# Stationary blocks of the feature projections laid out in interleaved pairs and read at a step of two, with moving operand and output traversed backwards

## What is computed

```python
# first block, two layers: a mixer and a convolved feed-forward, on 512 (later 256) tokens
q, k, v, u, g = jnp.split(h_lat @ w_in, splits, axis=-1)          # hybrid attention + gating
y_lat = jnp.concatenate([a_lat, s_lat], axis=-1) @ w_out
q, k, v, g = jnp.split(h_lat @ w_in, splits, axis=-1)             # retention
return (jax.nn.silu(g) * on.astype(g.dtype)) @ w_out
a = dwconv3(h @ w_in, conv_w, conv_b)                             # conv_ffn, D_FF = 2816
gate, up = jnp.split(a, 2, axis=-1)
return (jax.nn.silu(gate) * up) @ w_out

# second block, two layers on 272 tokens: mLSTM + LRU, differential attention, each with an MLP
h = h + _ab_mixer(hn, ab_w_in[j], ...)
h = h + _diff_attn(hn, c_w_in[j], ..., c_w_out[j], lambda_init)
a = jax.nn.relu(hn @ w1)
return (a * a) @ w2
```

## Time and profile before

| | us |
|---|---|
| median of 3 runs | 2000.32 |
| lowest, highest | 1997.08, 2002.23 |
| the profiled execution, whole | 2003.57 |
| its span, first to last instruction | 2001.8 |
| PE busy in it | 1907.4 |
| DVE busy in it | 1239.6 |
| ACT busy in it | 920.6 |

### The profile page before, as it was taken

The page is one execution under the profiler, slowest core; times in us unless marked ns, Lnnn a source line. Parts: engine busy times, 40 slices in busy tenths (PEclk is TensorE's granted clock), DMA queues, the critical chain, the costliest instruction groups (busy, mean ns, idle before and its releaser), DMA issues.

```text
span 2001.8 us, 33468 instructions
## 1 busy us (share of the span) xinstructions
PE 1907.4 (95%) x13373; PEld 1697.0 (85%) x13373; DVE 1239.6 (62%) x1853; ACT 920.6 (46%) x1441; POOL 229.6 (11%) x179
## 2 busy tenths in 40 slices
PE   5999979999999899999899998999999999989998
PEld 3776657778888589999889997998899999879997
DVE  6355355543664546677577768656875567787564
ACT  5344343322332422177475554357553445665453
POOL 2100104430552000022000000000010010000001
PEclk9999989999999999999999999999999999989999
DMA  9611465433222433222445553532345554224553
GB/s 389 239 61 64 168 232 185 166 115 113 91 85 93 183 125 107 89 101 85 168 153 177 198 177 128 176 134 91 127 169 181 177 172 145 95 95 169 192 187 127
DMA packets 43952, 296.79 MB, mean 148 GB/s; under 512 B 4976, under 2 KB 6129, under 8 KB 11697
## 3 DMA queue, kind: packets, MB, share of 16 engines
q1 hardware_dynamic: 36576, 247.48, 35.6%
q10 hardware_dynamic: 6048, 42.50, 5.9%
q0 software_dynamic: 1200, 5.02, 0.7%
HBM read 293.94 MB, written 1.05 MB: 147 GB/s over the span
## 4 chain that ended last, share of the span: by engine, by line
PE 83%; DVE 10%; ACT 4%; issue 2%; DMA 1%; POOL 1%; ACTq 0%; DVEq 0%; POOLq 0%
PE acc L462 23%; PE acc L463 23%; PE acc L464 22%; DVE w_lo L397 2%; PE acc L457 2%; PE acc L459 2%; PE acc L458 2%; PE wk L555 1%; PE wk L1733 1%; ACT w_hi L387 1%; PE acc L1722 1%; PE wk L1462 1%; DVE X L1073 1%; DVE nt L1079 1%; PE acc L1483 1%
## 5 line engine op out<-in xcount | busy, mean ns | idle before, releaser
L397 DVE TENSOR_TENSOR w_lo<-w_raw,w_hi 128x1024 fp32r<-128x1024 f32 (+2 forms) x472 | 574.3, 1255 | 177.2 <-ACT w_hi L387 175.6
L462 PE MATMUL acc<-Hhi,w_hi 128*128 128x272 f32 (+2 forms) x2048 | 654.1, 319 | 20.6 <-DVE Hlo L826 7.6
L387 ACT ACTIVATE w_hi<-w_raw 128x1024 fp32r<-128x1024 f32 (+2 forms) x472 | 452.4, 1005 | 424.3 <-PE acc L464 332.9
L463 PE MATMUL acc<-Hlo,w_hi 128*128 128x272 f32 (+2 forms) x2048 | 637.2, 311 | 0.0
L464 PE MATMUL acc<-Hhi,w_lo 128*128 128x272 f32 (+2 forms) x2048 | 635.8, 310 | 0.0
L462 PEld LDWEIGHTS acc<-Hhi,w_hi 128*128 128x128 f32 x2048 | 389.6, 190 | 67.8 <-issue 39.3
L464 PEld LDWEIGHTS acc<-Hhi,w_lo 128*128 128x128 f32 x2048 | 388.2, 190 | 19.5
L463 PEld LDWEIGHTS acc<-Hlo,w_hi 128*128 128x128 f32 x2048 | 389.1, 190 | 18.1
L462 PE MATMUL acc<-Fhi,w_hi 128*128 128x256 f32 (+2 forms) x864 | 262.6, 304 | 3.2 <-POOL Flo L1152 1.5
L464 PE MATMUL acc<-Fhi,w_lo 128*128 128x256 f32 (+2 forms) x864 | 261.9, 303 | 0.0
L463 PE MATMUL acc<-Flo,w_hi 128*128 128x256 f32 (+2 forms) x864 | 261.9, 303 | 0.0
(11 more groups left out here) (415 smaller groups left out, 2667.0 us busy)
## 6 DMA issues: line engine op xcount, KB each, us to landing
w_raw<-in_w_ffn_in SPq DMA_DIRECT2D x44, 1024.0 KB, 4.8
ada_ring<-in_w_ada ACTq DMA_DIRECT2D x40, 1024.0 KB, 5.8
w_raw<-in_w_mlp_in SPq DMA_DIRECT2D x32, 1024.0 KB, 4.8
w_raw<-in_w_mlp_out SPq DMA_DIRECT2D x32, 1024.0 KB, 4.8
w_raw<-in_w_ffn_out SPq DMA_DIRECT2D x32, 704.0 KB, 4.0
ada_first<-in_w_ada SPq DMA_DIRECT2D x8, 1024.0 KB, 20.4
w_raw<-in_w_ret_v SPq DMA_DIRECT2D x8, 1024.0 KB, 5.0
w_raw<-in_w_ret_g SPq DMA_DIRECT2D x8, 1024.0 KB, 4.7
```

The lines of the kernel that those rows point to most:

```text
L387: act.activation(w_hi[:, r, a:b], w_raw[:, r, a:b], ACT.Copy).then_inc(hi_done, 1)
L397: dve.tensor_tensor(w_lo[:, r, a:b], w_raw[:, r, a:b], w_hi[:, r, a:b].bitcast(F32), ALU.subtract).then_inc(lo_done, 1)
L462: pe.matmul(o, w_hi[:, r, w], x_hi(k), start=k == 0, stop=False)
L463: pe.matmul(o, w_hi[:, r, w], x_lo(k), start=False, stop=False)
```

## The change

For feature projections the host lays the blocks out in pairs: blocks 2i and 2i + 1 share 256 columns, the first on the even ones and the second on the odd ones (`_paired`). `stationary` reads a block back with a step of two elements, so that its 128 columns span 1024 bytes of a row in place of 512; a last block without a partner (K = 11, C = 1) stays as it was. In the same matmuls the moving operand and the output are given from the last column to the first, so each result lands where it did before. Projections of `kind` "tok" keep both. The number of instructions, their order on each engine, the semaphores, the transfers' sizes, the copies of ACT and DVE (still over contiguous halves) and all addresses are unchanged; only lines are renumbered (L462 to L464 become L470 to L472).

```diff
+        def stationary(w, r, p, j):
+
+            if j == p.K * p.C - 1 and j % 2 == 0:
+                return w[:, r, j * P:(j + 1) * P]
+            return w[:, r, j // 2 * 2 * P + j % 2:(j // 2 + 1) * 2 * P:2]
+
...
+                    if p.kind != "tok":
+                        o = o[:, ::-1]
...
-                        w = slice((k * p.C + c) * P, (k * p.C + c + 1) * P)
-                        pe.matmul(o, w_hi[:, r, w], x_hi(k), start=k == 0, stop=False)
-                        pe.matmul(o, w_hi[:, r, w], x_lo(k), start=False, stop=False)
-                        mm = pe.matmul(o, w_lo[:, r, w], x_hi(k), start=False, stop=k == last)
+                        b_hi, b_lo = stationary(w_hi, r, p, k * p.C + c), stationary(w_lo, r, p, k * p.C + c)
+                        pe.matmul(o, b_hi, x_hi(k)[:, ::-1], start=k == 0, stop=False)
+                        pe.matmul(o, b_hi, x_lo(k)[:, ::-1], start=False, stop=False)
+                        mm = pe.matmul(o, b_lo, x_hi(k)[:, ::-1], start=False, stop=k == last)
...
+def _paired(w, blocks):
+
+    n = w.shape[0]
+    pairs = w[:, :, :blocks // 2 * 2 * P].reshape(n, P, blocks // 2, 2, P).transpose(0, 1, 2, 4, 3)
+    return np.concatenate([pairs.reshape(n, P, -1), w[:, :, blocks // 2 * 2 * P:]], 2)
...
+    for p in PROJ:
+        if p.kind != "tok":
+            arrays["w_" + p.name] = _paired(arrays["w_" + p.name], p.K * p.C)
```

## The result

| | before | changed |
|---|---|---|
| median, us | 2001.28 (4 runs) | 2026.34 (4 runs) |
| lowest, highest | 1997.08, 2002.40 | 2025.84, 2026.68 |
| ratio | 1 | 1.0136, 95% interval 1.0118 to 1.0154 |
| profiled execution: span, us | 2001.8 | 2024.8 |

A forecast was written before the change was run, and what follows sets the result against it. PE's streaming was taken as the bound; gains of 10.3, 2.6, 2.4, 14.6 and 0.4 us summed to 30.3, step and reversal at zero. Keeping 30 gave 1970 us (chance 0.35), range 1910, less 2, to 2045, the forecast's own 1955 to 1990.

The forecast's parts named there:

- What bounds the kernel: Whole kernel: PE streams, busy 1907.4 of 2001.8 us with 83% of the chain, so the time is a sum of pitches.
- the price of 10.3 us for each ns: The three feature-projection matmuls, L462 to L464: each ns on the pitch of all 10320 was priced at 10.3 us.
- The source of the surplus: PE's matmuls: the 6 to 11% above array pace was put down to moving-operand reads colliding with the next weight load.
- The first rival: Feature matmuls: the whole gap to plain fp32's pace vanishes, 102 us of which 90 kept, 1910 us; chance 0.15.
- The step of two "at no cost of its own": Weight loads of feature matmuls: reading every second element was taken to add zero, hidden under the moving stream.
- The 1150 matmuls that ran at 113.4: 256-column matmuls in ffn1_in0 after its pause and both mlp1_out, taken as already at the good pace, with no gain.
- the third rival: Feature matmuls: loads touching twice the lines meet the stream more, +30 us and +5 us, 2035 us; chance 0.20.
- Equal pace keeps the streams apart: Load and moving stream, both over 1024 bytes per pitch at 256 columns, should stay apart; good pace everywhere, 30.3 us gained.
- The reversal "at zero": Feature matmuls: descending reads and accumulator writes touch the same bytes in the same number, so were priced at zero.
- The 512-wide matmuls: Feature matmuls of 512 columns: taken as already at the good pace, 226.6 ns; only 192 at 228.9 gain, 0.4 us.
- The fourth rival: Feature matmuls: the stationary read (+341 us, 2340 us) or the backward stream (+74 us) becomes the bound; chance 0.17.
- The two paces: 256-column matmuls: 113.4 and 117.8 ns for the same instructions, read as good and bad meetings; one pace, 113.4, expected afterwards.

## Why the prediction was wrong

**What bounds the kernel: right.** PE streams; both medians moved as its pitches did, and no other engine took or gave anything. The method of reading pitches from windows carried over to each experiment, and so did the price of 10.3 us for each ns on all 10320 matmuls.

**The source of the surplus: wrong, and this is the step on which the sign hung.** The prediction took all of the surplus over plain fp32's pace for meetings of the moving stream with the weight load. A plain fp32 matmul of 256 columns takes 3.45 / 16 = 0.216 us, nearly twice the time of an fp32r one, so it takes in moving columns at half the rate; it could not show what the fp32r stream costs by itself. Two experiments show more. With a load that walks nowhere the surplus stayed (228.7 ns), and with a moving operand that walks nowhere it went (215.9). Of the 13 ns above the array's 213.3, 11 come with the walk of the moving operand. Whether that walk costs them by itself or against any weight load, even one that does not walk, stays open. The first rival (the surplus goes entirely, 1910 us) had put its own counter-argument rightly: 226.6 looked like a property of the stream. It was less constant than it was taken for, though: the projections at 512 columns ahead of ffn0_in0 averaged 227.3 to 231.3 ns in the trace of before.

**The step of two "at no cost of its own": a term mis-sized.** The bound was written down, 110 ns for an open load, with the remark that from 3% more the 256-wide pitch follows it. These 110 ns are no measure of the load, only a ceiling: the matmuls in that row are plain fp32, and at the rate of the earlier trace rows 128 columns of it take 108 ns by themselves. With a moving operand of one element the step takes the pitch from 111.6 to 117.8, 5.6% more. The argument for zero was that the moving stream reads 1024 bytes in the time in which the load reads 512; but that is a contiguous read, and does not show what a read with a step costs. The 1150 matmuls that ran at 113.4 went to 117.8, which is the 5 us that the third rival had for them. In the changed kernel this can't be put down to the step alone, since the reversal alone brought them to 117.8 too.

**Equal pace keeps the streams apart: wrong.** With the step alone the 256-wide pitch is 119.9 ns, above the load's own 117.8 and above both paces of before, and at 512 columns, where the load is hidden nearly twice over, the stream slowed by 7 ns. If equal pace helped, the 256-wide pitch would have come down. Two streams do disturb each other here: the step of the load slows the 512-wide stream when it walks (233.5 ns) and not when it reads one element (215.9). But they disturb each other more at a wider span, not less.

**The reversal "at zero": wrong by 7 ns at 512 columns,** and by 4 ns at 256 in mlp1_out1 (113.5 to 117.8). It is the read of the moving operand; the write is free, as the prediction had it for both.

**The 512-wide matmuls were taken for immune.** They were given 0.4 us of the forecast, and the third rival, whose sign and size came nearest (2035 us, measured 2026), gave them next to nothing either. They carry 12.8 of the 24.9 us. So that rival's place was half wrong: it had the whole loss at 256 and 272 columns. Its mechanism, more meetings of the stream with a load that spans more, is what the step alone shows at 512.

**The fourth rival** priced a load at half as much again (2340 us). With a step of two and a moving operand of one element the load is the bound at 117.8 ns, 6 ns over the contiguous kernel and not 50; with a step of four it is the bound at about 233 ns, and the kernel took 2826 us. Its other half, 5% for reading backward, came out at 3% at 512 columns.

**The two paces.** The prediction expected a single pace afterwards, and there is a single one in both ffn1_in halves, but the slow one. That in the kernel before they come and go between executions is a guess: its median in the batches lay between 2000.4 and 2004.0 us with single runs from 1995.2 to 2007.6, while the four runs of the changed kernel lie within 0.9 us. Such a spread would fit, but no second trace of one kernel tests it.

**Still open** is why both edits together cost less (1.36%) than the step alone (1.5%). The traces show where: 117.8 ns against 119.9 at 256 columns, 126.3 against 127.5 at 272 (in mlp0_out both have 126.7). How the direction of the stream and the span of the load interact there was not tried apart. Nor was it settled why a step of two in the load slows a 512-wide stream by the same amount as a backward read, and both by no more.

## What to carry to other kernels

Before a surplus is put down to two streams that collide, take each away in turn, by an operand that reads one element over and over; two kernels of that kind show here that the surplus follows the moving operand, and that a step in the load costs time. As a working rule from these runs, a matmul's pitch is the larger of the stream's (226.6 ns for 512 fp32r columns, in proportion below) and the load's (at most 111.6 ns for 128 contiguous columns), with a few ns, up to 7, for their company; at 256 columns these are 2 ns apart, so anything that touches the layout of the stationary block has to be priced against the load as well. Keep fp32r stationary blocks contiguous and read the moving operand forward; the direction of the output was free here.

## What the runs showed of the hardware

- A weight block of 128 fp32r columns loads in at most 111.6 ns contiguous, 117.8 at a step of two (both with a moving operand of one element), about 233 at a step of four.
- A moving fp32r operand of 512 columns streams in 226.6 ns forward, 233.5 backward, and 215.9 where all columns are one element, each with a weight load of 128 columns beside it.
- A step of two in that load takes the forward stream to 233.5 ns, and leaves the stream of one element at 215.9.
- The output of a matmul may be written from the last column to the first at no cost (ratio 1.0000).
- A PE that is busy by its records can still lose its clock. In the two kernels with narrow matmuls the granted clock fell to 0.50, the level of 1.2 GHz, for long stretches, in which matmuls of 256, 64 and 64 columns took turns and PE's records covered all of the time. Part 2 of the page of the contiguous one, and a window of it (width, PE, PEld, DVE, ACT, POOL, PEclk):

```profile
PEclk7889778555565599955555555557955999975999
```

```profile
1150.00:1190.00 40.00, 40.00 (x190) 40.00 (x190) 18.17 (x30) 14.65 (x24) 0.00 (x0) 0.50 0.29 97
```

There a matmul costs 40 / 188 = 213 ns, against 114.0 at the full clock. Both kernels have less work for the array, and took 17 and 19% longer than the one before.
